# Block inverse carried as strictly lower part times T and its transpose, accumulated in PSUM, in one burst without weight ticks

## The reference

```
def step(state, inp):
    r_t, w_t, k_t, v_t, a_t, b_t = inp
    sa = jnp.einsum('bhij,bhj->bhi', state, a_t)
    state = (state * w_t[:, :, None, :] + sa[..., None] * b_t[:, :, None, :]
             + v_t[..., None] * k_t[:, :, None, :])
    return state, jnp.einsum('bhij,bhj->bhi', state, r_t)
```

## Time and profile before

| | |
|---|---|
| median of 3 runs | 2743.44 us (2741.64 to 2744.86) |
| span of the profiled execution | 2739.9 us |
| PE busy | 2669.7 us, 97% |
| DVE busy | 1729.0 us, 63% |
| ACT busy | 1220.3 us, 45% |
| POOL busy | 239.9 us, 9% |
| DMA | mean 153 GB/s |

### The profile page before, as it was taken

How to read it: one execution, slowest core, us unless ns; L and a number is a source line. 1 busy time by engine, 2 the same in 40 slices (tenths; PEclk the granted TensorE clock), 3 DMA queues, 4 the chain that set the end, 5 groups by cost and what they waited for, 6 DMA issues and landing times.

```text
span 2739.9 us, 50433 instructions
## 1 busy us (share of the span) xinstructions
PE 2669.7 (97%) x16843; PEld 2188.6 (80%) x16843; DVE 1729.0 (63%) x2858; ACT 1220.3 (45%) x1976; POOL 239.9 (9%) x341
## 2 busy tenths in 40 slices
PE   7999999999999999999899999999999999999998
PEld 6777777777888888888777777777778888888886
DVE  5766666656656656556567667666566565565665
ACT  5444444445434444444454444444454344344443
POOL 4111111100000000000022222221000000000000
PEclk9999999999999999999999999999999999999999
DMA  6333333355556555565533333333455655655554
GB/s 202 95 108 103 100 96 101 102 165 168 187 198 188 190 182 188 199 188 187 180 106 108 101 102 97 99 102 100 169 171 187 195 177 199 191 184 193 183 193 152
DMA packets 438043, 420.25 MB, mean 153 GB/s; under 512 B 19518, under 2 KB 351952, under 8 KB 437968
## 3 DMA queue, kind: packets, MB, share of 16 engines
q1 hardware_dynamic: 434320, 412.75, 48.1%
q0 software_dynamic: 3648, 6.52, 0.9%
HBM read 417.10 MB, written 2.10 MB: 153 GB/s over the span
## 4 chain that ended last, share of the span: by engine, by line
PE 91%; DVE 5%; issue 1%; ACT 1%; DMA 0%; DVEq 0%; SPq 0%; POOL 0%; ACTq 0%; POOLq 0%
PE gemm_bank L516 28%; PE gemm_bank L517 15%; PE gemm_bank L541 11%; PE gemm_bank L543 11%; PE gemm_bank L542 10%; PE gemm_bank L519 2%; PE mix_bank L698 2%; PE mix_bank L710 1%; PE mix_bank L707 1%; PE mix_bank L662 1%; DVE b_rn L1267 1%; PE mix_bank L728 1%; PE mix_bank L732 1%; PE mix_bank L742 1%; PE mix_bank L738 1%
## 5 line engine op out<-in xcount | busy, mean ns | idle before, releaser
L516 PE MATMUL gemm_bank<-b_hT,b_whi 128*128 128x512 f32 x3420 | 1267.0, 409 | 2.2 <-DVE b_zt L1162 2.2
L1156 DVE TENSOR_TENSOR b_wlo<-b_raw,b_whi 128x1024 fp32r<-128x1024 f32 x745 | 907.0, 1229 | 524.3 <-ACT b_whi L890 521.7
L890 ACT ACTIVATE b_whi<-b_raw 128x1024 fp32r<-128x1024 f32 x777 | 810.2, 1057 | 610.8 <-PE gemm_bank L543 421.2
L517 PE MATMUL gemm_bank<-b_hT,b_wlo 128*128 128x256 f32 x3648 | 1014.0, 282 | 0.0
L516 PEld LDWEIGHTS gemm_bank<-b_hT,b_whi 128*128 128x128 f32 x3420 | 643.4, 188 | 168.4 <-issue 22.4
L517 PEld LDWEIGHTS gemm_bank<-b_hT,b_wlo 128*128 128x128 f32 x3648 | 690.9, 189 | 14.8 <-issue 5.3
L541 PE MATMUL gemm_bank<-b_whi,b_mT 128*128 128x512 f32 x1280 | 502.9, 393 | 0.0
L543 PE MATMUL gemm_bank<-b_whi,b_mT 128*128 128x512 f32 x1280 | 498.4, 389 | 0.0
L542 PE MATMUL gemm_bank<-b_wlo,b_mT 128*128 128x512 f32 x1280 | 498.2, 389 | 0.0
L541 PEld LDWEIGHTS gemm_bank<-b_whi,b_mT 128*128 128x128 f32 x1280 | 240.3, 188 | 51.1 <-issue 1.7
L543 PEld LDWEIGHTS gemm_bank<-b_whi,b_mT 128*128 128x128 f32 x1280 | 240.3, 188 | 50.2
(11 more groups left out here) (242 smaller groups left out, 2287.0 us busy)
## 6 DMA issues: line engine op xcount, KB each, us to landing
b_raw<-in_w_up SPq DMA_DIRECT2D x256, 512.0 KB
b_raw<-in_w_down SPq DMA_DIRECT2D x256, 512.0 KB
b_raw<-in_w_in SPq DMA_DIRECT2D x384, 256.0 KB
b_raw<-in_w_out SPq DMA_DIRECT2D x60, 512.0 KB
b_raw<-in_w_in SPq DMA_DIRECT2D x8, 512.0 KB
b_xt<-in_x SPq DMA_DIRECT2D x4, 512.0 KB, 6.0
b_raw<-in_w_out SPq DMA_DIRECT2D x8, 256.0 KB
out<-b_xt SPq DMA_DIRECT2D x8, 256.0 KB, 2.4
```

Of the source, the lines that this page charges most:

```text
L516: mm(bank[b0 + b][:, :], whi[r][:, cols], pair, start=first, stop=False)
L517: m = mm(bank[b0 + b][:, 0:SEQ], wlo[r][:, cols], act[:, kt, 0, :], start=False, stop=False)
L890: f(whi[r][:, :], raw[r][:, :, :].rearrange("p a b -> p (a b)"), ACT.Copy).then_inc(hi_done, 1)
L1156: tt(wlo[r][:, :], flat(raw[r][:, :, :]), whi[r][:, :].bitcast(F32), ALU.subtract).then_inc(lo_done, 1)
```

## The change

The inverse is carried in another form. `mb[2 + w]` holds, in PSUM, Y = N T, which begins as N itself and is accumulated to over the levels; `mb[w]` holds Y transposed, loaded by a product with the identity and accumulated to as well. Level 0 goes through the same products as the others. In each level DVE masks Y out of PSUM into `X` (a multiply with `lvl`), ACT copies Y's transpose out into `YT`, and PE adds the level's products to both (`start=False`). PE waits for both, each with a `wait_alone`, for each w. At the end DVE adds the identity to give `TT`. There are 6 levels now, the predicated copies, the transposes of N, POOL's identity copies and 12 of the `fill(1)` calls are gone from this part, and no tick stands between the first product of the inverse and the first chunk.

What was threaded through the levels is moved. `finish(0)` is in DVE's level 1, and ahead of the `akv` copy on ACT. Gate products and the cosine half of the rotary go into DVE's later levels. `step(3)` to `step(7)` are moved into and behind the chunks, `finish(1)` from chunk 2 to behind the chunks, the sine half and the sum of the rotary from the levels to chunk 1, the scores from chunk 0 to behind all chunks, their mask and maxima with them. The ticks are handed out as 7, 4, 3, 2, 3 before the inverse, 2 in chunk 0, 3, 3 and 2 in chunks 1 to 3, then 3, the scores, 2, 3 behind the key norms, 2, 2, and the rest.

```
@@ PE mixer
-                fill(2)
+                fill(3)
...
-                    fill(2)
+                    fill(3 if u else 2)
 
                 pe.wait_ge(e["gram_ready"], 4 * n + 4)
-                for unit in range(4):
-                    m = turned(mb[2][:, P * unit:P * unit + P], G[:, unit, 2, :], ident)
-                m.then_inc(e["n_turned"], 1)
-                fill(1)
...
                 m.then_inc(e["akv_sum"], 1)
-                fill(1)
...
+                for u in range(2):
+                    for j in range(2):
+                        for h in range(2):
+                            hs = slice(HEAD * h, HEAD * h + HEAD)
+                            m = mm(y_cols(h, u)[halves[j ^ h], :], AR[hs, u, 0, halves[j ^ h]],
+                                   btl[hs, u, halves[j ^ h]], start=u == 0, stop=False, skip_group_check=True)
+                m.then_inc(e["n_sum"], 1)
+
+                for w in range(2):
+                    if w:
+                        wait_alone(pe, e["akv_out"], V)
+                    for u in range(2):
+                        for half in halves:
+                            mm(mb[w][half, CHUNK * u:CHUNK * u + CHUNK], ident[half, half], G[half, 2 * w + u, 2, half],
+                               start=u == 0, stop=False, skip_group_check=True)
+
+                for lv in range(LEVELS):
                     for w in range(2):
...
+                        wait_alone(pe, e["x_ready"], 2 * LEVELS * n + 2 * lv + w + 1)
+                        if lv:
+                            wait_alone(pe, e["yt_ready"], 2 * (LEVELS - 1) * n + 2 * lv + w - 1)
+                        for u in range(2):
+                            unit = 2 * w + u
+                            old = (lambda half: YT[half, unit, :]) if lv else (lambda half: G[half, unit, 2, half])
                             if lv < LEVELS - 1:
                                 for half in halves:
...
+                                    mm(blocks(y_cols(w, u)[half, :], lv, 0), old(half),
+                                       blocks(X[half, unit, :], lv, 0), start=False, stop=False, skip_group_check=True)
                             for half in halves:
...
+                                m = mm(mb[w][half, CHUNK * u:CHUNK * u + CHUNK], X[half, unit, :], old(half),
+                                       start=False, stop=lv == LEVELS - 1, skip_group_check=True)
+                        m.then_inc(e["lev_sum"], 1)
+
+                wait_alone(pe, e["tt_ready"], 2 * n + 2)
...
-                    fill(1)
+                    fill(1 if c else 2)
                     pe.wait_ge(e["u_out"], NCH * n + c + 1)
...
-                    if c == 0:
-
-                        pe.wait_ge(e["roped"], V)
-                        mm(mb[1][:, 0:P], qr[:, 0, 0:P], qr[:, 1, 0:P], start=True, stop=True)
...
-                    elif c < NCH - 1:
+                    if 0 < c < NCH - 1:
                         fill(1)
+
+                fill(3)
+                pe.wait_ge(e["roped"], V)
+                mm(mb[1][:, 0:P], qr[:, 0, 0:P], qr[:, 1, 0:P], start=True, stop=True)
...
+                fill(2)
 
                 pe.wait_ge(e["masked"], V)
...
                     key_norms(n + 1)
+                fill(3)
                 pe.wait_ge(e["probs"], V)
@@ ACT mixer
                 step(2)
                 step(3)
+                finish(0)
                 act.wait_ge(e["akv_sum"], V)
...
                 for lv in range(1, LEVELS):
                     for w in range(2):
...
+                        act.wait_ge(e["lev_sum"], 2 * LEVELS * n + 2 * lv - 1 + w)
+                        f(YT[:, 2 * w:2 * w + 2, :], mb[w][:, 0:P].rearrange("p (a b) -> p a b", a=2),
+                          ACT.Copy).then_inc(e["yt_ready"], 1)
...
+                    if c == 1:
+                        step(4)
+                    if c == 2:
+                        step(5)
+                    if c == 3:
+                        step(6)
+                        finish(1)
                         step(7)
@@ DVE mixer
+                gap = (None, lambda: finish(0), bonus_gate, norm_gate, lambda: rope_cos(0), lambda: rope_cos(1))
+                dve.wait_ge(e["n_sum"], V)
+                for lv in range(LEVELS):
+                    for w in range(2):
+                        if lv:
+                            dve.wait_ge(e["lev_sum"], 2 * LEVELS * n + 2 * lv - 1 + w)
+                        tt(X[:, 2 * w:2 * w + 2, :], mb[2 + w][:, 0:P].rearrange("p (a b) -> p a b", a=2),
+                           lvl[:, lv, :].unsqueeze(1).to_broadcast([P, 2, CHUNK]), ALU.mult).then_inc(e["x_ready"], 1)
+                    if lv:
+                        gap[lv]()
                 for w in range(2):
...
+                    dve.wait_ge(e["lev_sum"], 2 * LEVELS * n + 2 * LEVELS - 1 + w)
+                    tt(TT[:, 2 * w:2 * w + 2, :], mb[w][:, 0:P].rearrange("p (a b) -> p a b", a=2),
+                       cst[:, C_ID2:C_ID2 + CHUNK].unsqueeze(1).to_broadcast([P, 2, CHUNK]),
+                       ALU.add).then_inc(e["tt_ready"], 1)
...
+                    if c == 0:
+                        step(3)
                     if c == 1:
...
+                        tt(xs[:, :, :], xs[:, :, :],
...
+                        tt(qr[:, :, :], qr[:, :, :], xs[:, :, :], ALU.add).then_inc(e["roped"], 1)
                     if c == 2:
...
+                        step(4)
...
+                step(5)
+                finish(1)
+                step(6)
+                dve.wait_ge(e["score_sum"], V)
+                tt(sm[:, :], mb[1][:, 0:384], cst[:, C_CAUS:C_CAUS + 384], ALU.add).then_inc(e["masked"], 1)
+                dve.wait_ge(e["masked"], V)
+                nc.vector.tensor_reduce(small[:, 8:9], sm[:, 0:P], AX.X, ALU.max)
+                nc.vector.tensor_reduce(small[:, 9:10], sm[:, P:3 * P], AX.X, ALU.max).then_inc(e["smax"], 1)
+                dve.wait_ge(e["smax"], V)
+                ts(small[:, 10:12], small[:, 8:10], -SCALE, None, ALU.mult).then_inc(e["nmax"], 1)
                 if more:
                     key_norms(l, i + 1, n + 1)
+                step(7)
```

More of the change, by code:

```diff
@@ L690, in mixer @@
-                for lv in range(1, LEVELS):
-                    for w in range(2):
-                        if lv == 1 and w == 0:
-                            wait_alone(pe, e["akv_out"], V)
-                        wait_alone(pe, e["level_done"], 2 * LEVELS * n + (2 if lv == 1 else 2 * lv - 1 + w))
-                        for unit in (2 * w, 2 * w + 1):
-                            for half in halves:
-                                m = mm(packed(mb[2 + w][half, narrow(unit, half)], lv), G[half, unit, 2, half],
-                                       blocks(TT[half, unit, 0, half], lv, 0), start=True, stop=True)
-                        m.then_inc(e["x_sum"], 1)
-                    fill(1)
-                    for w in range(2):
-                        wait_alone(pe, e["x_out"], 2 * (LEVELS - 1) * n + 2 * lv - 1 + w)
-                        for unit in (2 * w, 2 * w + 1):
+                for u in range(2):
[4 more added lines that the diff above has]
+                                   btl[hs, u, halves[j ^ h]], start=u == 0, stop=False, skip_group_check=True)
@@ L709, in mixer @@
                             for half in halves:
-                                m = mm(packed(mb[w][half, narrow(unit, half, P)], lv), X[half, unit, half],
-                                       blocks(TT[half, unit, 1, half], lv, 1), start=True, stop=True)
-                        m.then_inc(e["t_sum"], 1)
-                    fill(1)
-                wait_alone(pe, e["level_done"], 2 * LEVELS * (n + 1))
+                                m = mm(mb[w][half, CHUNK * u:CHUNK * u + CHUNK], X[half, unit, :], old(half),
+                                       start=False, stop=lv == LEVELS - 1, skip_group_check=True)
@@ L1022, in mixer @@
                     if c == 0:
+                        act.wait_ge(tile_out, tiles + 2)
+                        for a, b in ((0, 64), (64, 0)):
+                            f(xs[a:a + 64, :, :], zt[b:b + 64, 3:5, 1:SEQ + 1], ACT.Copy).then_inc(e["swapped"], 1)
+                    if c == 1:
[5 more added lines that the diff above has]
+                        finish(1)
                         step(7)
-                    if c == 2:
-                        finish(1)
-                    if c == 3:
                         act.wait_ge(e["nmax"], V)
```

149 lines of the change are left out of this document (43 added, 106 removed).

## The result

| | before | after |
|---|---|---|
| median of 4 runs | 2744.15 us (2741.64 to 2745.95) | 2816.7 us (2800.82 to 2858.27) |
| span of the profiled execution | 2739.9 us | 2806.8 us |
| mean granted TensorE clock of it | 0.995 | 0.977 |

The changed kernel is slower, by a ratio of 1.0244 [1.0208, 1.0281]. Its four runs spread over 57 us, where those of before lie within 4, and the time goes with the clock: 2800.8 us at 0.980, 2808.5 at 0.977, 2824.9 at 0.969, 2858.3 at 0.956. The highest, 2% above the lowest, is not in the ratio. The profile is that of the run at 2808.5, so a gain counted against the median is 8 us larger than one counted against the profile.

The account below looks back on a forecast made before the run. TensorE, busy 97% of the span, was taken as the bound. -0.56 + 0.90 + 0.75 + 1.8 + 0.2 = +3.1 us in 14 mixers plus 0.4 twice gave +44 us: median 2788 us, range over the cases 2755 to 2828.

Parts of the forecast that it names:

- the slower rivals: Blocks not overlapping at 64 columns (chance 0.10, 2808 us) and the clock falling in the burst (0.12, 2815 or 2842).
- akv and levels, with the transposes: Inverse from akv to first chunk: 10.65 us against 11.21 without ticks, so -0.56 us a mixer.
- tail, interruptions with it: Tail: 1.8 us of waiting for the squared keys plus 0.2 for two more interruptions, a mixer.
- The level cycle: Inverse: one w from level to level takes 0.44 + 0.26 + 0.29 + 0.40 = 1.39 us, five times.
- The signs it gave: Inverse, in the profile: PE idle about 0.4 us ahead of each level group, released by DVE's masking.
- the rival that they don't: Inverse: diagonal blocks don't overlap at 64 columns, +1.3 us a mixer, 2808 us; chance 0.10.
- The levels are not hidden either: Rival, inverse: level waits hidden, a level 0.93 us instead of 1.39, total 2740 us; chance 0.12.
- 0.90 in chunk 0: Chunk 0: without the scores PE waits 0.90 us for the state, and the scores are paid later.
- 0.75 ahead of the value transposes: Tail: PE stands at 2.4 us, DVE's mask is done at 3.14, so PE waits 0.75 us.
- 1.8 ahead of the key sums: Tail: PE at 3.4 us waits until 5.2 for DVE's squared keys, 1.8 us.
- Forecast +0.4 each: Last mixer of each layer, no key norms or finish(1): -0.56 + 0.90 + 0.1 = 0.4 us, twice.
- the clock falls in the burst: Rival: PE's waits in the inverse halve the clock, up to 1.7 us in each of 16 mixers, 2815 us; chance 0.12.

Follow-up runs that it names:

- the edit of its order: The changed kernel with DVE's step(6) moved from ahead of the mask to behind the key norms, nothing else; 2820.94 us, ratio 1.0261 to before.
- putting them back: POOL's eight identity copies and DVE's wait restored in the new inverse with ticks between its levels (2701.33 us); 2708.93 us.
- the one tick moved back: The changed kernel with fill(4) for fill(3) behind the key norms, so the last flush holds 6 ticks, not 7; 2841.7 us, ratio 1.039.
- the added products: The changed kernel with unread products behind levels 2 to 5 and ahead of the waits for the mask and the key sums; 2766.82 us, ratio 1.0089.
- useful ticks in the same places: The new inverse with ticks between its levels and everything else placed as before the change; 2701.33 us, ratio 0.9854 to before.

## Why the prediction was right, and where it was not

The forecast was 2788 us and the range 2755 to 2828; the median is 2816.7. Sign and range held, but the sum that gave 2788 did not: most of its terms were good, things outside them were missed, and a rival came true on top. It had 44 us of structure and none of clock; the profiled execution has 24.2 and 42.7. That the two errors offset each other in part is luck; the range reached as far as the median because the slower rivals were in it. Of the 20 us of structure that did not come, the last mixer of each layer is 9 together, the starts of the mixers are 5 (9.5 gained in layer 0, 4.6 lost in layer 1), the inverse is 3.5, and 2 I can't assign.

| us a mixer | predicted | layer 0 | layer 1 |
|---|---|---|---|
| akv and levels, with the transposes | -0.56 | -0.88 | -0.74 |
| chunks and wait for the mask | +1.65 | +1.57 | +1.63 |
| tail, interruptions with it | +2.0 | +2.05 | +2.05 |
| start, up to the `t1` sum | 0 | -1.54 | +0.95 |
| period | +3.1 | +1.15 | +3.8 |

(Stretches of after less those of before, each added tick at 0.706, where the clock holds. The start of +0.95 and the period of +3.8 in layer 1 are those of the five mixers that meet POOL; the other two gain 0.16 at most at the start. The last line is read from the periods.)

- **The inverse.** The level cycle was forecast as 1.39 us and is 1.39; masking 0.29 as taken, 0.38 through two waits for 0.40. The signs it gave were not all right: PE is idle 0.17 to 0.26 us, not 0.4, and once a level from level 1 on; the second group follows without a wait, and the trace names issue and not the masking. The identity products of the two blocks (L686, 64 columns) run two in 0.058 us, which one such product alone takes among the U products of the earlier trace rows. So the columns overlap, and the rival that they don't is false; both blocks write one PSUM bank, so the rule of PSUM pressure named there does not bind here. In the level groups a pair of them takes 0.07 to 0.09, and a group of 16 spans 0.46 for 0.44. The levels are not hidden either.
- **Chunks and tail.** 0.8 for 0.90 in chunk 0, 0.80 for 0.75 ahead of the value transposes, 1.76 for 1.8 ahead of the key sums. That the queue on DVE sets both of the last is shown by the edit of its order: the first goes, and the key sums come 1.1 us earlier.
- **POOL.** "POOL's eight identity copies [...] save nothing now" is the step that failed. They had lengthened a DVE operation on the chain to the `t1` sum from 0.48 to 1.32 us: PE waited there 9.8 us in all. It is shown by putting them back, +7.6 us, 1.0 of the 1.54 at the start of layer 0. The other 0.5, and the loss at layer 1, come from the flush of 7 ticks, which the sum took as free: it shifts DVE against POOL's splits, out of one in layer 0 (0.28 us for 0.76) and into one in layer 1 (2.46). That the shift is the cause is shown by the one tick moved back: 7.2 us at layer 0, 7.1 at layer 1.
- **The last mixers.** Forecast +0.4 each; they are 4.7 and 3.7 us shorter, with what follows them. Their waits are constants and their inverse takes 9.14, the start is 0.9 shorter at layer 0, and no tail wait stands in them. The remaining 2 us or so I can't assign.
- **The clock.** This is the rival "the clock falls in the burst", to which I gave 0.12. It came with 42.7 us of the profiled run, more than the structure's 24.2. The prediction's own sign of being wrong, halves in the clock row inside the mixers, is there. It is shown by the added products: 42 us back from the profiled run, with more work done. The rival's 2815 for 2816.7 is luck as well: it stood on the same 44 us of structure and on 27 us of clock. The place was half right. It falls behind the burst, where the gaps are of 0.5 us at most and one of 0.8 follows in chunk 0, and the rival had no falls in the tail at all, where eight came. Against it I had put that PE works more than half of the time in the burst; it works 86% of it by the records and the clock fell all the same. The Trainium skill, TensorE: Matmul & The Clock Gate, "A second HAM failure mode: psum-queue depth-cycling", describes another kernel, whose PE micro-idles between groups of matmuls often enough for the clock to go back and forth between its two levels; the second mixer of after agrees (1.00 in its inverse, 0.50 for 30.7 us behind it), and I should have weighed that sentence and not only the one on idling.

So 2788 was nearer than the sum deserved: without the clock the kernel is at about 2765, 23 us below the forecast, by the runs' own line and by the run with added products (2766.8).

## What to carry to other kernels

A burst of dependent products without filler pays each round trip, and may pay again in the granted clock: look at the clock row of the stretches behind it, and at whether the runs spread. The new algebra, with POOL's copies gone (about 8 us of it), was worth 40 us, and the arrangement that came with it cost 107 against the profiled run and 115 against the median: try them one at a time. Where waits can't be filled with work, products that nobody needs can be cheaper than the silence, but useful ticks in the same places are worth far more (2701 against 2767 us). Compute the values of two successive waits ahead of both, if PE is early there.

## What the runs showed of the hardware

- A TENSOR_SCALAR of 128 x 256 f32 on DVE takes 0.28 us, and 2.46 when it starts just behind the start of a 2.4 us TENSOR_TENSOR on POOL: it ends 0.15 us behind that one, and so does one that starts in the middle of the split (0.6 to 0.8 us long). The RECIPROCAL of that size beside it isn't held, 1.75 us either way. The Trainium skill, GPSIMD Engine Reference, "1. Specifications", says that POOL's SBUF interfaces are shared with VectorE, with contention for DVE instructions in a 2-port mode or with two SBUF inputs; the 1.32 us for 0.48 of the operation with two inputs agree, and the one with a single input agrees if it runs in such a mode, which no run here shows.
- The clock can stay at 1.2 GHz for 30.7 us, and once for 34.1, with PE busy 97 and 98% of them, and came back both times in the three ticks behind the last chunk. Moving one DVE operation changed which mixers it hits, and so did moving a single tick (25 us more by the medians). With work that nobody needs in the burst's waits, or with PE idle for 0.6 us of the inverse instead of 1.5, it did not fall behind the burst in any mixer.
- The spread of the runs was itself a sign: 57, 41, 41 and 19 us in the four kernels with long stretches behind the burst, 2 to 6 us in the others.
